# One decoder layer in float32 halves: the order of the products in a tile, the entry of the FFN and the early loads

## The reference

```python
mod = silu(c) @ w_ada + b_ada                 # six vectors of 2048
sh_m, sc_m, ga_m, sh_f, sc_f, ga_f = split(mod, 6)
h = rmsnorm(x, g_pre_mix) * (1 + sc_m) + sh_m
# token_mixer: h @ w_in, both branches, then
merged = sigmoid(gate_a) * (o @ w_o_hg) + sigmoid(gate_b) * (att @ w_o_mla)
y = merged @ w_out
x = x + ga_m * rmsnorm(y, g_post_mix)
h = rmsnorm(x, g_pre_ffn) * (1 + sc_f) + sh_f
gate, up = split(h @ w_gate_up, 2)
x = x + ga_f * rmsnorm((silu(gate) * up) @ w_down, g_post_ffn)
```

## Time and profile before

| what | value |
|---|---|
| median of 3 runs | 1890.21 us (1888.95 to 1891.62) |
| the profiled execution | 1886.96 us |
| its span, first to last instruction | 1885.1 us |
| PE busy | 1822.5 us, 97% of the span |
| weight loads of PE | 1529.7 us, 81% |
| DVE, ACT, POOL busy | 1296.2, 891.3, 104.3 us |
| DMA | 423.38 MB, mean 225 GB/s |

### The profile page before, as it was taken

The page is one execution under the profiler, slowest core; times in us unless marked ns, Lnnn a source line. Parts: engine busy times, 40 slices in busy tenths (PEclk is TensorE's granted clock), DMA queues, the critical chain, the costliest instruction groups (busy, mean ns, idle before and its releaser), DMA issues.

```text
span 1885.1 us, 24326 instructions
## 1 busy us (share of the span) xinstructions
PE 1822.5 (97%) x8828; PEld 1529.7 (81%) x8828; DVE 1296.2 (69%) x1361; ACT 891.3 (47%) x1007; POOL 104.3 (6%) x72
## 2 busy tenths in 40 slices
PE   3999999999999999999999989999999999999997
PEld 2788888888888888888778867888888888888886
DVE  7799768678668668669677554666656666665557
ACT  5544555645645645644334446444443444443443
POOL 0000000120120120220000000000000000000000
PEclk9999999999999999999999999999999999999999
DMA  9997548646646647547786654666666666665553
GB/s 383 409 366 254 191 156 291 237 162 227 233 156 231 226 156 244 180 167 268 242 317 226 219 179 138 223 222 230 212 227 230 212 222 219 228 212 176 193 190 131
DMA packets 115985, 423.38 MB, mean 225 GB/s; under 512 B 13008, under 2 KB 13392, under 8 KB 115408
## 3 DMA queue, kind: packets, MB, share of 16 engines
q1 hardware_dynamic: 115920, 422.51, 65.3%
HBM read 420.36 MB, written 2.10 MB: 224 GB/s over the span
## 4 chain that ended last, share of the span: by engine, by line
PE 89%; DVE 5%; DMA 4%; issue 1%; ACT 1%; SPq 0%; POOL 0%; DVEq 0%; ACTq 0%; POOLq 0%
PE PS L839 27%; PE PS L841 26%; PE PS L840 26%; DMA ada_raw<-in_ada 2%; PE PS L986 2%; DVE ada_acc L1232 2%; DMA raw<-in_w_start 2%; PE PS L848 1%; DVE wlo L1225 1%; PE PS L874 1%; PE PS L1032 1%; PE PS L1031 1%; PE PS L1143 0%; PE PS L857 0%; PE PS L866 0%
## 5 line engine op out<-in xcount | busy, mean ns | idle before, releaser
L1225 DVE TENSOR_TENSOR wlo<-raw,whi 128x1024 fp32r<-128x1024 f32 x600 | 732.5, 1223 | 415.7 <-ACT whi L465 414.2
L465 ACT ACTIVATE whi<-raw 128x1024 fp32r<-128x1024 f32 x600 | 630.1, 1053 | 743.2 <-PE PS L841 658.3
L839 PE MATMUL PS<-whi,hT_hi 128*128 128x512 f32 x1792 | 707.6, 395 | 8.6 <-DVE wlo L1225 5.4
L841 PE MATMUL PS<-whi,hT_lo 128*128 128x512 f32 x1792 | 699.1, 390 | 0.0
L840 PE MATMUL PS<-wlo,hT_hi 128*128 128x512 f32 x1792 | 698.7, 390 | 0.0
L839 PEld LDWEIGHTS PS<-whi,hT_hi 128*128 128x128 f32 x1792 | 337.3, 188 | 77.9 <-issue 6.0
L841 PEld LDWEIGHTS PS<-whi,hT_lo 128*128 128x128 f32 x1792 | 336.9, 188 | 71.1
L840 PEld LDWEIGHTS PS<-wlo,hT_hi 128*128 128x128 f32 x1792 | 337.4, 188 | 67.4 <-issue 0.2
L839 PE MATMUL PS<-whi,cT_hi 128*128 128x512 f32 (+1 forms) x592 | 231.5, 391 | 2.0 <-DVE side L1549 1.5
L840 PE MATMUL PS<-wlo,cT_hi 128*128 128x512 f32 (+1 forms) x592 | 227.9, 385 | 0.0
L841 PE MATMUL PS<-whi,cT_lo 128*128 128x512 f32 (+1 forms) x592 | 227.9, 385 | 0.0
(11 more groups left out here) (228 smaller groups left out, 1052.0 us busy)
## 6 DMA issues: line engine op xcount, KB each, us to landing
ada_raw<-in_ada SPq DMA_DIRECT2D x142, 512.0 KB, 4.8
raw<-in_w_gate SPq DMA_DIRECT2D x88, 512.0 KB, 4.1
raw<-in_w_up SPq DMA_DIRECT2D x88, 512.0 KB, 4.2
raw<-in_w_down SPq DMA_DIRECT2D x88, 512.0 KB, 4.1
raw<-in_w_start SPq DMA_DIRECT2D x80, 512.0 KB, 4.9
raw<-in_w_hf SPq DMA_DIRECT2D x32, 512.0 KB, 3.9
raw<-in_w_hq SPq DMA_DIRECT2D x32, 512.0 KB, 5.0
raw<-in_w_hi SPq DMA_DIRECT2D x32, 512.0 KB, 4.5
```

What stands on the lines that cost most here:

```text
L465: nc.scalar.activation(whi[:, pl.slot(c), 0:w], raw[:, pl.slot(c), 0:w], ACT.Copy)\
L839: nc.tensor.matmul(o, hi[:, kt, tok], whi[:, s, cols], start=start, stop=False)
L841: last = nc.tensor.matmul(o, lo[:, kt, tok], whi[:, s, cols], start=False, stop=stop)
L1225: nc.vector.tensor_tensor(wlo[:, s, 0:w], raw[:, s, 0:w], whi[:, s, 0:w].bitcast(F32), ALU.subtract)\
```

## The change

1. `multiply` now does, for each chunk, the eight products with `whi` first, behind a wait for the high half alone, and then the four with `wlo`, behind a wait for the low half. The number of matmuls stays.
2. The last four chunks of out are multiplied in two passes, token tile 0 and then token tile 1 (`multiply_rows`); so are the first four of the FFN. Squares, rms, x2 and the diagonal are formed for one token tile at a time, x2 in two halves of 1024 columns. Blocks 0 to 3 of the transposed h are made in units of one token tile (`H2`), so there are 12 units in place of 8.
3. SP asks for `ada0` pieces three ahead of their due chunk at first (`ADA_FIRST`), one more for every three chunks up to ten; the loads of `w_kr` and the masks move behind chunk 24.
4. `ADA_OH` starts at step 6 in place of 4 and is spread to step 26. PE's sums move from step 23 to 25 (om) and 26 (oh), DVE reads them at 27 and 28, and om's go to another bank.

```diff
-            for a in range(KD, KD + ADA_SLOTS):
+            asked = KD + ADA_FIRST
+            for a in range(KD, asked):
                 load_ada0(a)
-            sp.dma_start(key_weights, w_kr).then_inc(sig("kr_loaded"), 16)
-            sp.dma_start(msk[:], masks).then_inc(sig("masks_loaded"), 16)
...
-                    for a in range(KD + ada_due(c - RING) + ADA_SLOTS, KD + ada_due(c - RING + 1) + ADA_SLOTS):
-                        if a < ADA0:
-                            load_ada0(a)
+                    ahead = KD + ada_due(c - RING + 1) + min(ADA_SLOTS, ADA_FIRST + (c - RING) // 3)
+                    for a in range(asked, min(ahead, ADA0)):
+                        load_ada0(a)
+                    asked = max(asked, min(ahead, ADA0))
...
-        ADA_OH = [4, 5, 6, 7, 8, 9, 10, 12, 13, 14, 15, 17, 18, 20, 21, 22]
+        ADA_OH = [6, 7, 8, 9, 10, 13, 14, 15, 17, 18, 21, 22, 23, 24, 25, 26]
...
+        H2 = [(kp, slice(tt * P, (tt + 1) * P)) for tt in range(TT) for kp in range(4)] + [(kp, slice(0, T)) for kp in range(4, KP)]
...
             # multiply
-                    pe.wait_ge(lo_ready, pl.through(c0 + c))
                     s = pl.slot(c0 + c)
+                    pe.wait_ge(hi_ready, pl.through(c0 + c))
                     for tt in range(TT):
                         for k in range(KC):
...
-                            nc.tensor.matmul(o, hi[:, kt, tok], whi[:, s, cols], start=start, stop=False)
-                            nc.tensor.matmul(o, hi[:, kt, tok], wlo[:, s, cols], start=False, stop=False)
-                            last = nc.tensor.matmul(o, lo[:, kt, tok], whi[:, s, cols], start=False, stop=stop)
+                            nc.tensor.matmul(o, hi[:, kt, tok], whi[:, s, cols], start=c == 0 and k == 0, stop=False)
+                            nc.tensor.matmul(o, lo[:, kt, tok], whi[:, s, cols], start=False, stop=False)
+                    pe.wait_ge(lo_ready, pl.through(c0 + c))
+                    for tt in range(TT):
+                        for k in range(KC):
...
+                            last = nc.tensor.matmul(PS[:, 2 * p + tt, 0:width], hi[:, kt, tok], wlo[:, s, cols],
+                                                    start=False, stop=c == n - 1 and k == KC - 1)
...
             # PE, end of out and entry of the FFN (multiply_rows: the same order for one token tile)
+            for tt in range(TT):
+                for kp in range(CD - RING, CD):
+                    hi, lo, home = row_home(2 * KP + kp)
+                    last = multiply_rows(pl, GD - 1, CD, (GD - 1) * CD, kp, tt, hi, lo, kt0=KC * (home - kp))
...
+            for u in range(4):
+                transpose_x2(u)
+            for c in range(4):
+                if c == 3:
+                    for u in range(4, 8):
+                        transpose_x2(u)
                 pe.wait_ge(sig("h2_low"), c + 1)
+                multiply_rows(first, 0, CD, 0, c, 0, hT_hi, hT_lo)
+            for c in range(4):
+                pe.wait_ge(sig("h2_low"), 4 + c + 1)
+                multiply_rows(first, 0, CD, 0, c, 1, hT_hi, hT_lo).then_inc(multiplied, 1)
+                transpose_x2(8 + c)
+            for c in range(4, CD):
+                pe.wait_ge(sig("h2_low"), 4 + c + 1)
                 multiply(first, 0, CD, 0, c, c + 1, hT_hi, hT_lo)
...
             # ACT
+            square_out_rows(0)
+            high(first, 0)
+            high(first, 1)
+            square_x2(0, 0)
+            square_x2(0, 1)
+            square_out_rows(1)
+            high(first, 2)
+            h2_high(0)
+            h2_high(1)
+            square_x2(1, 0)
+            h2_high(2)
+            square_x2(1, 1)
+            h2_high(3)
+            high(first, 3)
...
             # DVE
+            y_rms(0)
...
+            mix_x2(0, 0)
+            mix_x2(0, 1)
+            low(first, 0)
+            x2_rms(0)
+            y_rms(1)
...
+            mix_x2(1, 0)
+            low(first, 1)
+            h2_low(0)
+            mix_x2(1, 1)
+            h2_low(1)
+            low(first, 2)
+            h2_low(2)
+            x2_rms(1)
+            h2_low(3)
+            low(first, 3)
```

More of the change, by code:

```diff
@@ L706, in square_out @@
                       .then_inc(sig("y_squared"), 1)
-            for c in range(GD * CD + AHEAD):
+            for c in range(GD * CD):
                 high(pl, c)
@@ L717, in _, with square_out_rows @@
                     copy_gain(0)
-            for tt in range(TT):
-                act.wait_ge(sig("x_mixed"), tt + 1)
+            first = Place(B_FF, G_FF)
+            junk = side[:].rearrange("p t c -> p (t c)")
+            def square_out_rows(tt):
                 if tt:
[L722 to L727, removed]
+                    act.wait_ge(multiplied, pl.through(N_ST - 1))
+                    act.wait_ge(sig("x2_squared"), 2)
+                else:
+                    act.wait_ge(sig("out_rows"), 1)
+                act.wait_ge(sig("y_squared"), (GD - 1) * TT + tt)
+                nc.scalar.activation(junk[:, 0:NW], PS[:, 2 * pl.pair(GD - 1) + tt, :], ACT.Square,
+                                     accum_out=sums[:, tt, GD - 1:GD]).then_inc(sig("y_squared"), 1)
@@ new lines, in _ @@
+            square_out_rows(0)
[13 more added lines that the diff above has]
+            for u in range(4, 8):
+                h2_high(u)
+            for u in range(8, len(H2)):
+                high(first, u - 4)
+                h2_high(u)
@@ L1124, in _, with multiply_rows @@
             pl = place_out
-            for c in range(N_ST):
+            def multiply_rows(pl, g, n, c0, c, tt, hi, lo, kt0=0):
+                p = pl.pair(g)
+                if c == 0 and tt == 0:
+                    pe.wait_ge(pair_free[p], pl.freed(g))
+                s = pl.slot(c0 + c)
+                pe.wait_ge(hi_ready, pl.through(c0 + c))
+                tok = slice(tt * P, (tt + 1) * P)
+                o = PS[:, 2 * p + tt, :]
+                for k in range(KC):
+                    kt = kt0 + c * KC + k
+                    cols = slice(k * NW, (k + 1) * NW)
+                    nc.tensor.matmul(o, hi[:, kt, tok], whi[:, s, cols], start=c == 0 and k == 0, stop=False)
+                    nc.tensor.matmul(o, lo[:, kt, tok], whi[:, s, cols], start=False, stop=False)
+                pe.wait_ge(lo_ready, pl.through(c0 + c))
+                for k in range(KC):
+                    last = nc.tensor.matmul(o, hi[:, kt0 + c * KC + k, tok], wlo[:, s, k * NW:(k + 1) * NW],
+                                            start=False, stop=c == n - 1 and k == KC - 1)
+                return last
+            for c in range(N_ST - RING):
                 if c == CD:
@@ L1132, in _, with transpose_x2 @@
                     transpose_rows(23)
+            for tt in range(TT):
+                for kp in range(CD - RING, CD):
+                    hi, lo, home = row_home(2 * KP + kp)
+                    last = multiply_rows(pl, GD - 1, CD, (GD - 1) * CD, kp, tt, hi, lo, kt0=KC * (home - kp))
+                    if tt:
+                        last.then_inc(multiplied, 1)
+                if tt == 0:
+                    last.then_inc(sig("out_rows"), 1)
             pe.wait_ge(sig("gain_copied"), 2)
-            def transpose_x2(kp):
-                if kp >= 4:
-                    pe.wait_ge(sig("h2_scaled"), 2 * (kp - 3))
+            def transpose_x2(u):
+                kp, tok = H2[u]
+                if u >= 4:
+                    pe.wait_ge(sig("h2_scaled"), 2 * (u - 3))
                 for j in range(2):
-                    for tt in range(TT):
+                    for tt in range(tok.start // P, tok.stop // P):
                         if kp == 0 and j == 0:
@@ L1703, in hidden @@
+            for u in range(8, len(H2)):
+                low(first, u - 4)
+                h2_low(u)
             def hidden(pl, c=-1, g=-1):
```

134 lines of the change are left out of this document (80 added, 54 removed).

## The result

The changed kernel takes **1868.51 us** in the median of 4 runs (1868.17 to 1869.41), the kernel before, timed beside it, 1889.58 (1888.45 to 1891.62): a ratio of 0.9888, 95% interval 0.9871 to 0.9905, or 21.1 us less. Forecast were 15.6 us less and 1874.6, within 1868.5 to 1882; the median stands at the lower edge of that. The profiled execution of after took 1869.41 us, with a span of 1867.6. Against the profiled execution of before (1886.96) that is 17.5 us less. So there are two gaps to explain: 1.9 us from profile to profile, and 3.5 more from median to median.

The account below looks back on a forecast made before the run. PE, busy 1822.5 of 1885.1 us, was taken as the bound. Start 3.96, om 1.62, oh 3.4 and entry 6.6 sum to 15.6 us, taking the median from 1890.21 to 1874.6 us, range 1868.5 to 1882.

Parts of the forecast that it names:

- rival A: The second wait costs time in each of 600 chunks, 0.08 us each: slower by 32 us, 1922; chance 0.06.
- Elsewhere 0: High half first gains 0 outside the named places, since PE waits for no low half there.
- Gain 1.62; bounds 0 and 1.62: om stage: moving the sum from behind step 23 to behind 25 removes PE's wait for the last piece; 1.62 us.
- oh, 3.4: oh stage: all three PE stops behind the reload of x go; 3.4 us, bounds 1 and 3.7.
- rival D: oh stops again, its 1.4 us margin being used up by x: 1878 us; chance 0.09.
- 8.5, less 1.9 for the clock. Entry 6.6: FFN entry: chunk 4 starts 8.5 us earlier, less 1.9 for slow matmuls; net 6.6 us, bounds 3 and 9.5.
- 24 to 25: Sign for the entry: from the end of out to the FFN's chunk 4, 24 to 25 us in place of 32.
- rival C: The entry gives 3 us or less, by clock or one more link in DVE's line: 1878 to 1880; chance 0.15.
- 3.16 + 0.80: Start: the stop before chunk 4 (3.16 us) and the wait at the second quarter's sum (0.80) go.
- a load is asked for six to seven chunks ahead of its use, 16 us, so it is covered: Start: DMA falls behind 0.27 us a chunk, 5.7 us over some 21 chunks, but the 16 us lead covers it.
- rival B: The start keeps its loss, later or elsewhere, as early DMA time is missing at chunks 10 to 20: 1878.6; chance 0.1.
- The median stands 3.25 above that execution: Conversion to the median: before's median is 3.25 us above its profiled execution, giving 1890.21 - 15.6 = 1874.6 us.

Follow-up runs that it names:

- e4: Kernel before with only the product order changed, high-half products first and a second wait before the low-half ones: median 1885.09 us, ratio 0.9983.
- e5: e4 with both waits repeated before each low product, 7 more waits in each of 596 chunks: median 1895.23 us, ratio 1.0037.
- e8: Kernel before with om's step alone: row sums after step 25 instead of 23, into another bank, DVE's piece one later: median 1884.99 us, ratio 0.9983.
- e0: The kernel before, unchanged, profiled again: median 1889.05 us, ratio 1.0002, profiled execution 1886.05 us.
- e3: Kernel before with only the FFN entry and out's last four chunks done by token tile: median 1879.01 us, ratio 0.9948.
- e6: The changed kernel with the old early loads put back: median 1871.76 us, ratio 0.9914 to the kernel before.
- e10: e7 timed again beside the changed kernel: median 1868.21 us, ratio 0.9893 to the kernel before.
- e11: e7 with the second quarter's row sums one group of two chunks later: median 1866.66 us, ratio 0.9890 to the kernel before.
- e7: The changed kernel with early loads held back less, 5 pieces ahead at first and one more every 2: median 1867.59 us, ratio 0.9892 to the kernel before.
- e9: The changed kernel, unaltered, timed and profiled again: median 1868.28 us, ratio 0.9891 to the kernel before.
- e2: Kernel before with only the new steps of pieces and sums in om and oh: median 1882.00 us, ratio 0.9965.
- e1: Kernel before with only the new order of early loads: median 1886.45 us, ratio 0.9991.

## Why the prediction was right and wrong

**Direction and mechanisms** were right: every stop that it named went, and the pace stayed. Two terms were too small, one was too large in the profile, and one conversion was wrong. Forecast and measurement lie 5.5 us apart. From profile to profile the start gave 3.9 less than forecast, om and oh 3.1 more and the entry 2.7 more, together 1.9; the conversion to the median gave 3.5. That the terms of the start and of the entry nearly cancel is luck.

**Pace, rival A.** Right. e4 is not slower but 2.9 us faster, and e5 puts a passed wait at 2.4 ns or less. The Trainium skill, "TensorE: Matmul & The Clock Gate", section "Architectural detail", has the queue pulling weight loads ahead of running matmuls; the 0.23 us across the new wait and e4's time agree that a passed wait does not prevent it. "Elsewhere 0" is neither borne out nor refuted: e4's 2.9 us are not located.

**om, "Gain 1.62; bounds 0 and 1.62".** Mis-sized, at half: 3.1 us measured (e8, profiles), 3.65 by medians. I counted the stop and not the clock that fell behind it, though in the start I had named just this pattern (a rest, small sums, then matmuls 0.42 apart). The upper bound was not a bound. The rows right behind the earlier trace rows show it.

**oh, 3.4.** The remainder of the stretch is 6.2 less 3.1, so 3.1, against e0, and 8.1 less 3.2 (1.62 + 1.6), so 4.9, against before, where the starts around the first stop in oh lie 2.17 us apart and 0.90 in e0. Right, with the size within what two executions differ; the thin margin of 1.4 us held, and rival D is out.

**Entry, "8.5, less 1.9 for the clock. Entry 6.6".** The working of 8.5 was right to 0.6 us at its end (28.1 against 28.7 for chunk 4), and so was each step before it. From the end of out to chunk 4 PE now takes 22.7 us, against 31.8: 9.1 less. (The sign "24 to 25" was missed on the good side; the working itself has 28.7 less 5.4, 23.3.) The failed step is the 1.9 for the clock, charged on top. The clock did fall in four of seven profiled executions of the new entry (e3, e6, e10, e11: 0.57 or 0.58 over four us) and in three it did not (after, e7, e9), and the stretch from spread to last is 811.9 in six of them and 812.2 in e3. The working had PE waiting 2.5 us for DVE before chunk 0; slower transposes use up that wait first, and by chunk 0 the clock was back (0.99 or 1.00). So it cost nothing that can be told. The old entry has no such wait behind its transposes and does pay: its clock was back after four us in before and e4 (stretches of 821.2 and 821.3) and later in the five others (821.9 to 822.2). 9.3 to 10.2 in place of 6.6; rival C is out.

**Start, "3.16 + 0.80".** Half right by its mechanism, wrong by its result in the profile. No stop before chunk 4, and the second quarter's sum 2.5 us earlier: as computed. Then the failed step of this term: "a load is asked for six to seven chunks ahead of its use, 16 us, so it is covered". Chunk 4 was asked for at 34.90, as computed, but SP's next requests are tied to the next low halves, and these came only at 41.02 and 44.81, since DVE waited 2.11 us for PE's sums and 1.82 for ACT and then had work of its own between them. With only three pieces ahead the DMA rested in 39:52, and the lead was never built; PE stopped for 0.84 and 1.04 some 65 us later. (In e7 and e10 the low halves come at the same distances, but more pieces are asked for, and the DMA does not rest.) That is rival B, in a part that I had given 0.1, and e7 and e10 show it by taking it away: 2.5 and 2.0 us in the profiles. Against before's mark the term measured 0.1 (after) and 0.9 (e9) of its 3.96, and 2.6 and 2.9 with the loads of e7 and e10.

**"The median stands 3.25 above that execution"**, and so it would after. This step failed by the most: the conversion from profile to median. The profiled executions of before are quick ones (0.993, 0.992) out of runs that spread over 5 us; after's stands 0.9 above its median. The profiles show two things that before's was spared and most executions of the old kernel were not: the fall of the clock near 82 us (five of eight have it, 1.4 to 3.2 us) and the later return of the clock in the old entry (five of seven, some 0.8 us). The changed kernel has the first in none of its profiles, and its entry hides the second. Beside it before's median moved from 1890.21 to 1889.58 with a fourth run, so before stands 2.6 above its profiled execution and after 0.9 below: 3.5 of the 21.1 us are this. The parts alone bear it out by their medians: 3.15 + 7.6 + 10.6 = 21.3, with e4's 2.9 lying in part over the same stops in oh as e2's.

Shown are the om term, the entry's hidden clock loss, and the DMA's rest as the cause of the new stops. Only argued is that the new loads prevent the fall of the clock near 82 us because PE no longer rests before those sums: e10 rests there for about 0.9 us and its clock stays at 1.00 in the profile, and e10 still has both kinds of run. What its longer runs lose is open.

## What to carry to other kernels

A short stop of PE followed by very small matmuls can cost twice what the waits list says, in some executions and not in others: read the starts of the ten matmuls behind it before pricing its removal, and profile more than one execution. A loss of clock just ahead of a wait costs nothing until that wait is used up, so do not add it to a working that has PE waiting there. Before turning a profiled execution into a median, look where it lies among all runs, by time and by granted clock; a median well above the profile is itself a loss that a change can remove. Loads that are held back so that the first ones come sooner must be let go before the DMA rests, for a DMA that idles early is paid for tens of microseconds later.

## What the runs showed of the hardware

The same instructions with the same stop of 0.64 us near 82 us were followed by a clock of 1.00, 1.00, 1.00 in one program's execution and by 0.76, 0.50, 0.89 in another's, with 20 and 11 matmuls started in the middle 4 us. Over the 58 runs of before beside the experiments the time falls with the mean granted clock, on average 1890.9, 1889.5, 1888.5, 1886.5 and 1886.4 us at 0.989 to 0.993, but runs at one value differ by up to 4.5 us, and the changed kernel's do not follow it (1867.81 at 0.995, 1868.64 at 0.997). The Trainium skill, "TensorE: Matmul & The Clock Gate", section "What's actually happening", says that the number of slow matmuls at a start varies from run to run of one kernel and puts the loss below 1% of a typical span; here it is up to 3 us of 1887, 0.2%, and it can follow a stop in mid kernel as well as a start.

The same holds for the new entry. A rest of 2.22 us and 16 transposes of 128 columns left the clock at 1.00 in after and brought it to 0.57 in e6; and 1.1 us of rest and 16 sums of one column brought it to 0.73 over 908:912 in e0 and left it at 1.00 in e1. So one execution in which the clock holds does not show that a stop is harmless, and these runs do not tell what decides it.
